# Up weights summed by adding transfers, with plain first blocks, in a two-layer decoder step

## The chip, the cores and the metric

The kernel runs on one core of one Trainium2 chip. It is written instruction by instruction, with semaphores. The metric is the device time of one execution in microseconds: 2723.18 us, the median of three runs (2722.01 to 2725.67).

## The reference, cut to what matters

Two decoder layers are applied to 520 tokens (512 of a prompt, 8 samples), with d_model 1024, all in fp32. Each layer has two FFNs of width 2816, and all four are of this form:

```
h = rmsnorm(x, gain)
x = x + 0.5 * (silu(h @ w1) * (h @ w3)) @ w2
```

Between them stand one input projection, a gated DeltaNet branch, a differential attention branch, a gated merge and an output projection; a per-layer embedding gate ends the layer. The change touches only the FFNs and what prepares x for them, so the rest is left out here.

## The kernel before

**Numbers.** TensorE works on float32r. For full precision each operand is split into a high part (a copy by ACT, rounded to float32r) and a low part (VectorE: value less high), and every product is three matmuls: high x high, high x low, low x high. Activations lie feature by feature on the partitions, so a matmul has a 128 x 128 weight and 260 of the 520 tokens.

**The up stage with seven products.** For one block n of 128 hidden features (22 blocks, KF), w1 and w3 are taken together. Features are cut into an even and an odd half, tokens into two halves: a 2 x 2 by 2 x 2 product. It is computed with seven products and sums of the operands in place of eight (Winograd's form of Strassen). Each product is 4 x 3 = 12 matmuls, so a block is 84 (`up_block`, `up_product`, L730, L742). It needs seven weight matrices of 128 x 512: four arrive (`up_blocks`, L2552) and three or four are sums; and seven matrices of x, sums of the four scaled quarters (`pair_act`, `pair_dve`, L1317 to L1360, into HA and HB).

**One block's way.** `WF[n % 2]` (weven or wodd, L196) holds four slots `w` and three slots `v`. SP loads 1 MB in two transfers (L465) as soon as `split_done` says that block n-2 has its last low part. GpSimd makes two sums (`up_sums`, L1794), VectorE two more (L1907). ACT makes the high parts UHa (in two steps) and UHb (`up_high`, L1386), VectorE the low parts ULa and ULb (`up_low`, L1897); the end of ULb counts `split_done`. TensorE waits for ULa before products 0 and 2 and for ULb before product 4 (`up_waits`, L718). ACT copies partial results out of PSUM (`up_out`, L1405); VectorE adds them to the rest and multiplies by R, the reciprocal root of the norm (`up_u`, `up_v`), ACT applies SiLU, VectorE forms G (`up_g`), ACT its high part and GpSimd its low part (`gate_low`, L1811) for blocks up to 10; for the later ones GpSimd does it after the sums of the last block.

VectorE's order in a block is written out in `ffn` (L1937):

```
up_u(n-1); up_low(n, 2); up_v(n-1); up_low(n+1, 0); up_g(n-1); up_low(n+1, 1); up_sums(n+1)
```

**Start of an FFN.** `up_begin` (L747) runs the first three products of block 0 over feature pairs as x becomes ready, waiting for `hx_raw` and `hx_all`; then comes `norm_sum`, the sum of squares over features by a matmul with ones, and the rest of block 0.

**Down stage.** 16 weight chunks of 128 x 1408 are loaded, split and multiplied with Gh and Gl (L645, `product`); VectorE adds half the result to X.

Of the kernel before, what the change touches and what calls it, by code (L numbers as in the profile page):

```python
# [14 lines left out]
P = 128  # L15
# [127 lines left out]
def hybrid_trunk(nc, A, O):  # L143
    ctx = ExitStack()
    with ctx:
# [37 lines left out]
        acc = at("acc", [P, T], F32, odd_at + 3 * 2048)  # L183
        gap_at = top.at
# [23 lines left out]
        HA, HA0 = (at(n, [P, 8, 4, HT], dt, h_at) for n, dt in (("HA", R32), ("HA0", F32)))  # L208
        HB, HB0 = (at(n, [P, 6, 4, HT], dt, g_at + GE * T * 4) for n, dt in (("HB", R32), ("HB0", F32)))
# [125 lines left out]
        up_sum, up_sum2, up_hi, up_lo, up_form, up_copy = (sem(n) for n in ("up_sum", "up_sum2", "up_hi", "up_lo", "up_form", "up_copy"))  # L335
# [107 lines left out]

        def half_t(c):
            return slice(c * HT, (c + 1) * HT)
# [4 lines left out]
        def _(sp_):  # L450
# [7 lines left out]
            def ffn(L, nb, up, down, hid):  # L458
                for n in range(KF):
                    if n == 1:  # L460
                        sp_.wait_ge(block_done, L * NB + nb + FREE)
                    else:
                        sp_.wait_ge(split_done, L * NB + nb + (n or 1) + 1)
                    for q in range(2):
                        sp_.dma_start(WF[n % 2][q][:, 0:3:2, :],  # L465
                                      up[L, n][:, 1024 * q:1024 * (q + 1)].rearrange("p (a c) -> p a c", a=2)
                                      ).then_inc(raw_ready[n % 2], 16)
                for n in range(2 * KD):
                    sp_.wait_ge(split_done, L * NB + nb + KF + (n if n > 1 else 0) + 1)
                    if n == 1:  # L470
                        sp_.wait_ge(up_sum, 2 * (up_first(L, hid) + KF) - 1)
# [162 lines left out]
        def _(pe):  # L634
# [64 lines left out]
            def norm_sum(L, nj):  # L699

                if L == 0 and nj == 0:
                    pe.wait_ge(loads, 16)
                pe.wait_ge(acc_ready, L * NH + KD * (nj + 1))
                for c in range(2):
                    last = nc.tensor.matmul(ps[:, 6 + c, 0:HT], ones, acc[:, c * HT:(c + 1) * HT], start=True, stop=True)
                last.then_inc(sum_ready, 1)
# [5 lines left out]
            WH = [UHa[:, f, :] for f in range(4)] + [UHb[:, f, :] for f in range(3)]  # L712
            WL = [ULa[:, f, :] for f in range(4)] + [ULb[:, f, :] for f in range(3)]
            XH = [HA[:, 1], HA[:, 0], HA[:, 3], HB[:, 0], HB[:, 1], HA[:, 2], HB[:, 2]]
            XL = [HA[:, 5], HA[:, 4], HA[:, 7], HB[:, 3], HB[:, 4], HA[:, 6], HB[:, 5]]
            BANK = (2, 3, 1, 2, 3, 0, 2)

            def up_waits(L, nb, ub, nj, hid, n, p, f):  # L718
                g = up_first(L, hid)
# [3 lines left out]
                elif f == 2:  # L723
                    pe.wait_ge(up_lo, 2 * n + (2 * g + 2))
                elif f == 4:
                    pe.wait_ge(split_done, n + (L * NB + nb + FREE + 1))
                if f in (3, 4, 6):
                    pe.wait_ge(up_copy, 4 * n + (4 * g + {3: 1, 4: 2, 6: 3}[f]))

            def up_product(p, f, i0=0, i1=4, before=None):  # L730
                for i in range(i0, i1):
                    if before:
                        before(i)
                    w = slice(i * P, (i + 1) * P)
                    for t, (a, x) in enumerate(((WH[f], XH[f]), (WH[f], XL[f]), (WL[f], XH[f]))):
                        last = nc.tensor.matmul(ps[:, 4 * p + BANK[f], 0:HT], a[:, w], x[:, i, :],  # L736
                                                start=f in (0, 1, 2, 5) and i == 0 and t == 0, stop=i == 3 and t == 2,
                                                skip_group_check=True)
                if i1 == 4:
                    last.then_inc(block_done if f == 6 else up_form, 1)  # L740

            def up_block(L, nb, ub, nj, hid, n, p):  # L742
                for f in range(7):
                    up_waits(L, nb, ub, nj, hid, n, p, f)
                    up_product(p, f)

            def up_begin(L, nb, ub, nj, hid):  # L747
                x = 4 * (2 * L + hid)

                def raw_part(i):  # L750
                    pe.wait_ge(hx_raw, x + i + 1)

                def all_part(i):
                    pe.wait_ge(hx_all, x + i + 1)

                for f in range(3):
                    up_waits(L, nb, ub, nj, hid, 0, 0, f)
                    up_product(0, f, 0, 3, all_part if f == 1 else raw_part)
                for f in range(3):
                    up_product(0, f, 3, 4, all_part if f == 1 else raw_part)  # L760
                norm_sum(L, nj)
                for f in range(3, 7):
                    up_waits(L, nb, ub, nj, hid, 0, 0, f)
                    up_product(0, f)
                pe.wait_ge(rt_ready, L * NORMS + (nj + 1))
                up_block(L, nb, ub, nj, hid, 1, 1)

            def ffn(L, nb, ub, nj, hid):
                up_begin(L, nb, ub, nj, hid)
                with pe.Fori(1, KF // 2) as i:  # L770
                    for p in range(2):
                        up_block(L, nb, ub, nj, hid, 2 * i + p, p)
# [505 lines left out]
            for c in range(2):  # L1278
                pe.wait_ge(half_evac2, c + 1)
                pe.wait_ge(acc_ready, DEPTH * NH - 1)  # L1280
                nc.tensor.matmul(ps[:, 6 + c, 0:HT], ones, acc[:, c * HT:(c + 1) * HT], start=True, stop=False)
# [35 lines left out]
        def pair_act(act, L, nj, hid, i):  # L1317

            n = 4 * (2 * L + hid) + i
            if i:  # L1320
                act.wait_ge(hx_all, n)
            for q in range(2):
                nx = nc.scalar.activation(HA0[:, 4 + 2 * q:6 + 2 * q, i, :], halves(X[:, 2 * i + q, :]), ACT.Copy,
                                          scale=gain(L, nj, 2 * i + q))
            nx.then_inc(hx_gain, 1)
            act.drain()
            nc.scalar.activation(HA[:, 1:4, i, :], HA0[:, 5:8, i, :], ACT.Copy).then_inc(hx_hraw, 1)

        def pair_squares(act, L, nj, hid, i):
            act.wait_ge(acc_ready, L * NH + KD * nj + 2 * i)  # L1330
            for q in range(2):
                nc.scalar.activation(ta[:, q, :], X[:, 2 * i + q, :], ACT.Square).then_inc(sq_ready, 1)

        def pair_sums_act(act, L, nj, hid, i):
            act.wait_ge(hx_sum, 4 * (2 * L + hid) + i + 1)
            nc.scalar.activation(HA[:, 0, i, :], HA0[:, 4, i, :], ACT.Copy)
            nc.scalar.activation(HB[:, 0:3, i, :], HB0[:, 3:6, i, :], ACT.Copy).then_inc(hx_hsum, 1)

        def pair_dve(dve, L, nj, hid, i):

            V = nc.vector
            n = 4 * (2 * L + hid) + i + 1
            s1, x11, x22, x12 = (HA0[:, 4 + k, i, :] for k in range(4))
            s2, s4, s3 = (HB0[:, 3 + k, i, :] for k in range(3))
            dve.wait_ge(hx_gain, n)
            V.tensor_tensor(s3, x11, s1, ALU.subtract)
            V.tensor_tensor(s1, s1, x22, ALU.add)
            dve.drain()
            V.tensor_tensor(s2, s1, x11, ALU.subtract)
            dve.drain()  # L1350
            V.tensor_tensor(s4, x12, s2, ALU.subtract).then_inc(hx_sum, 1)
            dve.wait_ge(hx_hraw, n)
            dve.drain()
            V.tensor_tensor(HA[:, 5:8, i, :], HA0[:, 5:8, i, :], HA[:, 1:4, i, :].bitcast(F32), ALU.subtract  # L1354
                            ).then_inc(hx_raw, 1)
            dve.wait_ge(hx_hsum, n)
            dve.drain()
            V.tensor_tensor(HA[:, 4, i, :], s1, HA[:, 0, i, :].bitcast(F32), ALU.subtract)
            V.tensor_tensor(HB[:, 3:6, i, :], HB0[:, 3:6, i, :], HB[:, 0:3, i, :].bitcast(F32), ALU.subtract
                            ).then_inc(hx_all, 1)  # L1360

        def pair_sums_dve(dve, L, nj, hid, i):
            for q in range(2):
                dve.wait_ge(sq_ready, L * NH + KD * nj + 2 * i + q + 1)
                nc.vector.tensor_tensor(acc[:, :], acc[:, :], ta[:, q, :], ALU.add).then_inc(acc_ready, 1)
                dve.drain()

        @block.scalar
        def _(act):
# [9 lines left out]
            def norm_root(L, nj):  # L1379
                act.wait_ge(sum_ready, L * NORMS + (nj + 1))  # L1380
                A_(halves(R[:, :]), pair(6), ACT.Sqrt, scale=1.0 / D, bias=eps).then_inc(rt_ready, 1)
# [3 lines left out]

            def up_high(L, nb, hid, n, g):  # L1386

                b = up_first(L, hid)
                if g == 2:
                    act.wait_ge(block_done, L * NB + nb + n - 1 + FREE + 1)  # L1390
                elif n:
                    act.wait_ge(up_form, 6 * (b + n - 1) + 2 * g + 2)
                else:
                    act.wait_ge(block_done, L * NB + nb + 1)
                if g == 2:
                    act.wait_ge(up_sum2, b + n + 1)
                else:
                    act.wait_ge(up_sum, 2 * (b + n) + g + 1)
# [6 lines left out]
            def up_out(L, nb, nj, hid, n, f):  # L1405

                p = n % 2
                if f == 6:
                    act.wait_ge(block_done, L * NB + nb + n + FREE + 1)
                else:  # L1410
                    act.wait_ge(up_form, 6 * (up_first(L, hid) + n) + f + 1)
                if f == 0:
                    if n < 2:
                        act.wait_ge(acc_ready, L * NH + KD * (nj + 1))
                    else:
                        act.wait_ge(g_ready, up_first(L, hid) + n - 1)
# [1219 lines left out]
```

## Time and profile before

| | us |
|---|---|
| median of 3 runs | 2723.18 |
| profiled execution | 2725.64 |
| its span | 2723.8 |
| TensorE busy | 2603.0 (96%) |
| VectorE busy | 1933.8 (71%) |
| ACT busy | 1185.9 (44%) |
| GpSimd busy | 542.2 (20%) |

Stages of the profiled execution, by the span's clock: FFN 1 from 16.84 (down products from 273.09), FFN 2 to about 1320 (down from 1172), FFN 3 from 1367 (down from 1621), FFN 4 to about 2667 (down from 2520). In the profile an engine's busy time counts its instructions alone; the chain follows the work that ended last; "releaser" names what ended an idle time. VectorE's sums and low parts all have line L1882, a helper, and are told apart by their tiles. A matmul's own duration overlaps the next one's, so the pace of TensorE is read from counts over time.

### The profile page before, as it was taken

To read this page: it belongs to the slowest core of one execution; us is meant where nothing else is said; L and a number is where in the kernel's file an instruction comes from. 1 tells how busy PE (TensorE), PEld (TensorE's weight loads), DVE (VectorE), ACT (ScalarE), POOL (GpSimd) and SP (SyncE) were. 2 spreads that over 40 slices of the span, in tenths; PEclk is the share of its full clock that TensorE was granted. 3 is DMA by queue.
4 is the path that set the end of the run, shared out by engine and by line. 5 is a ranking of instruction groups with operands and counts; after the bars stand their busy time and mean duration, and the time that the engine had idled before them with its cause. 6 is when DMAs were issued, how large, how long until landed. Compare 5 with 4: busy or idle time off the path is not lost.

```text
span 2723.8 us, 54467 instructions
## 1 busy us (share of the span) xinstructions
PE 2603.0 (96%) x22804; PEld 2447.8 (90%) x22804; DVE 1933.8 (71%) x2315; ACT 1185.9 (44%) x1674; POOL 542.2 (20%) x326
## 2 busy tenths in 40 slices
PE   5999999999999899999979999999999998999997
PEld 5999999976699899999969999999757998999997
DVE  7999437665676799953689993476566668999436
ACT  5555323423663555532355552244236535555323
POOL 1432200332000143320024331003220002432300
PEclk9999999999999999999989999999999999999999
DMA  3232332268422123332212232322783222233231
GB/s 106 95 101 99 96 120 99 81 225 285 147 84 88 63 93 100 101 111 83 92 64 93 93 104 97 120 96 94 257 277 107 91 80 69 95 99 106 96 99 64
DMA packets 142109, 304.38 MB, mean 112 GB/s; under 512 B 14946, under 2 KB 25186, under 8 KB 141410
## 3 DMA queue, kind: packets, MB, share of 16 engines
q1 hardware_dynamic: 141922, 301.79, 33.5%
q8 instruction: 129, 2.11, 0.3%
q14 instruction: 58, 0.48, 0.1%
HBM read 290.30 MB, written 11.44 MB: 111 GB/s over the span
## 4 chain that ended last, share of the span: by engine, by line
PE 72%; DVE 14%; DVEq 10%; ACT 2%; issue 2%; ACTq 0%; POOLq 0%
PE ps L645 33%; PE ps L736 14%; PE ps L693 14%; DVEq L1919 4%; DVEq L1925 3%; DVE ta L1882 3%; DVE ULa L1882 2%; DVE tb L1882 2%; PE ps L909 2%; DVEq L1929 2%; DVE G L1882 1%; PE ps L1001 1%; DVE weven L1882 1%; DVE wodd L1882 1%; PE ps L1020 1%
## 5 line engine op out<-in xcount | busy, mean ns | idle before, releaser
L645 PE MATMUL ps<-Gh,ring 128*128 128x260 f32 x2816 | 453.7, 283 | 0.0
L736 PE MATMUL ps<-HA,UHa 128*128 128x260 f32 x2112 | 391.7, 286 | 59.9 <-DVE HA L1354 38.0
L736 PEld LDWEIGHTS ps<-HA,UHa 128*128 128x128 f32 x2112 | 330.2, 191 | 63.1 <-DVE HA L1354 30.5
L645 PEld LDWEIGHTS ps<-Gh,ring 128*128 128x128 f32 x2816 | 386.0, 188 | 0.0
L693 PE MATMUL ps<-Hh,ring 128*128 128x260 f32 x2048 | 342.3, 286 | 0.1
L736 PE MATMUL ps<-HA,ULa 128*128 128x260 f32 x1056 | 301.0, 285 | 0.0
L693 PEld LDWEIGHTS ps<-Hh,ring 128*128 128x128 f32 x2048 | 285.2, 188 | 4.3 <-issue 2.7
L1802 POOL TENSOR_TENSOR weven<-weven,weven 128x512 f32<-128x512 f32 x88 | 136.0, 1546 | 749.8 <-DMA weven<-in_ffn_up 742.7
L645 PE MATMUL ps<-Gl,ring 128*128 128x260 f32 x1408 | 282.6, 282 | 0.0
L736 PE MATMUL ps<-HB,UHb 128*128 128x260 f32 x1408 | 270.3, 289 | 7.1 <-DVE ULb L1882 7.1
L1882 DVE TENSOR_TENSOR ring<-rawd,ring 128x1408 fp32r<-128x1408 f32 x64 | 110.3, 1724 | 190.0 <-ACT ring L1371 190.0
L1371 ACT ACTIVATE ring<-raw 128x2048 fp32r<-128x2048 f32 (+1 forms) x72 | 134.4, 1866 | 236.5 <-PE ps L645 131.9
L736 PEld LDWEIGHTS ps<-HB,UHb 128*128 128x128 f32 x1408 | 218.2, 190 | 14.0 <-DVE ULb L1882 7.4
L1371 ACT ACTIVATE ring<-rawd 128x1408 fp32r<-128x1408 f32 x64 | 88.3, 1380 | 312.5 <-PE ps L645 312.5
L645 PEld LDWEIGHTS ps<-Gl,ring 128*128 128x128 f32 x1408 | 217.3, 188 | 0.0
L1813 POOL TENSOR_TENSOR Gl<-G,Gh 128x520 fp32r<-128x520 f32 x88 | 144.0, 1658 | 341.0 <-ACT Gh L1371 341.0
L693 PE MATMUL ps<-Hl,ring 128*128 128x260 f32 x1024 | 205.7, 282 | 0.0
L736 PEld LDWEIGHTS ps<-HA,ULa 128*128 128x128 f32 x1056 | 202.5, 192 | 0.0
L645 PE MATMUL ps<-Hh,ring 128*128 128x260 f32 x1248 | 201.6, 282 | 0.0
L736 PE MATMUL ps<-HB,ULb 128*128 128x260 f32 x704 | 200.3, 284 | 0.0
L1802 POOL TENSOR_TENSOR wodd<-wodd,wodd 128x512 f32<-128x512 f32 x88 | 137.6, 1563 | 253.7 <-DMA wodd<-in_ffn_up 191.4
L645 PEld LDWEIGHTS ps<-Hh,ring 128*128 128x128 f32 x1248 | 171.0, 188 | 0.2
(322 smaller groups left out, 5617.3 us busy)
## 6 DMA issues: line engine op xcount, KB each, us to landing
weven<-in_ffn_up SPq DMA_DIRECT2D x88, 512.0 KB, 4.7
wodd<-in_ffn_up SPq DMA_DIRECT2D x88, 512.0 KB, 4.9
rawd<-in_ffn_down SPq DMA_DIRECT2D x128, 352.0 KB, 3.4
kb<-in_cache_k SPq DMA_DIRECT2D x128, 256.0 KB, 4.0
kb<-in_cache_v SPq DMA_DIRECT2D x128, 256.0 KB, 4.0
raw<-in_w_in SPq DMA_DIRECT2D x56, 512.0 KB, 4.7
raw<-in_w_gate SPq DMA_DIRECT2D x32, 512.0 KB, 4.6
raw<-in_w_ab SPq DMA_DIRECT2D x16, 512.0 KB, 4.3
```

Of the source, the lines that this page charges most:

```text
L645: last = nc.tensor.matmul(ps[:, bank + 2 * m + c, 0:HT], w, x[:, k0 + k, c * HT:(c + 1) * HT], start=starts and k == 0 and n == 0, stop=st ...
L693: last = nc.tensor.matmul(ps[:, 2 * m + c, 0:HT], w, x[:, k, c * HT:(c + 1) * HT], start=k == 0 and t == 0, stop=k == KD - 1 and t == 2)
L736: last = nc.tensor.matmul(ps[:, 4 * p + BANK[f], 0:HT], a[:, w], x[:, i, :], start=f in (0, 1, 2, 5) and i == 0 and t == 0, stop=i == 3 an ...
L909: last = nc.tensor.matmul(ps[part(h % 2), bank, cell(x, h)], lhs[part(h % 2), cell(x, h)], rhs(part(h % 2), cell(x, h)), start=x == 0 and ...
L1001: last = nc.tensor.matmul(ps[32 * h:32 * h + 32, 6, :].rearrange("p (g k) -> p g k", g=4), qz[:, s * P + 32 * h:s * P + 32 * h + 32], kb[t ...
L1371: return nc.scalar.activation(out, in_, func, **kw)
L1802: nc.gpsimd.tensor_tensor(part_of(o), part_of(a), part_of(b), ALU.subtract).then_inc(up_sum, 1)
L1813: nc.gpsimd.tensor_tensor(Gl[:, n, :], G0[:, n, :], Gh[:, n, :].bitcast(F32), ALU.subtract).then_inc(gl_done, 1)
L1882: return V.tensor_tensor(out, a_, b_, op)
L1919: dve.drain()
L1925: dve.drain()
L1929: dve.drain()
```

## The change

1. The first block of each FFN (the first three of the first FFN) is computed with eight plain products over single feature chunks: `up_plain`, 96 matmuls. x for it is only scaled and split (`raw_act`, `raw_dve`: XR, XT). The sums for the other blocks (HS) are formed beside it (`form_scaled`, `form_sums`, `form_high`, `form_low`).
2. In the other blocks the order and signs of the products change, so that u is complete in PSUM: ACT copies two partial results into other PSUM banks instead of SBUF. `up_u` is one multiplication by R. `up_v` is one operation without R; R is multiplied in after the down products, with the factor -0.5.
3. The weight sums: SP loads the first quarter a second time, into slot `w[:, 1]`. GpSimd then issues two accumulating transfers, which add the fourth quarter to `w[:, 1]` and the third to `v[:, 2]`. VectorE waits for both (`added`) and makes the two other sums, the second from the first. GpSimd makes no weight sums of its own.
4. In VectorE's order `up_sums(n+1)` moves from the end of the block to a place ahead of `up_low(n, 2)`.

The core of the diff:

```
             def ffn(L, nb, up, down, hid):          # SP
                     for q in range(2):
                         sp_.dma_start(WF[n % 2][q][:, 0:3:2, :], ...).then_inc(raw_ready[n % 2], 16)
+                        if q == 0 and n >= plain(L, hid):
+                            sp_.dma_start(WF[n % 2][0][:, 1, :], up[L, n][:, 0:512]).then_inc(first_load[n % 2], 16)
...
+            def add_parts(L, nb, hid, n, up):       # GpSimd
+                w, v = WF[n % 2]
+                pool.wait_ge(raw_ready[n % 2], (L * NB + nb + n) // 2 * 32 + 32)
+                pool.wait_ge(first_load[n % 2], 16 * formed_alike(L, hid, n))
+                pool.dma_start(w[:, 1, :], up[L, n][:, 1536:2048], accum_op=ALU.add).then_inc(added[n % 2], 16)
+                pool.dma_start(v[:, 2, :], up[L, n][:, 1024:1536], accum_op=ALU.add).then_inc(added[n % 2], 16)
+
+            def ffn(L, nb, hid, up):
+                np = plain(L, hid)
+                add_parts(L, nb, hid, np, up)
+                add_parts(L, nb, hid, np + 1, up)
                 for n in range(KF):
-                    up_sums(L, nb, hid, n)
-                    if 2 <= n < GE + 2:
-                        gate_low(L, hid, n - 2)
+                    if 0 < n <= GE:
+                        gate_low(L, hid, n - 1)
+                    if n >= np and n + 2 < KF:
+                        add_parts(L, nb, hid, n + 2, up)
...
+            def up_sums(L, nb, hid, n):             # VectorE
+                w, v = WF[n % 2]
+                dve.wait_ge(added[n % 2], 32 * formed_alike(L, hid, n))
+                TT(w[:, 3, :], w[:, 1, :], v[:, 0, :], ALU.add).then_inc(up_sum, 1)
+                dve.drain()
+                TT(v[:, 1, :], w[:, 3, :], w[:, 2, :], ALU.add).then_inc(up_sum, 1)
...
             def up_u(L, nb, hid, n):
                 done(L, nb + n)
-                dve.wait_ge(up_copy, 4 * (up_first(L, hid) + n) + 4)
-                u = halves(ta[:, n % 2, :])
-                TT(u, pair(4 * (n % 2)), u, ALU.add)
-                dve.drain()
-                TT(ta[:, n % 2, :], ta[:, n % 2, :], R[:, :], ALU.mult).then_inc(ta_ready, 1)
+                TT(halves(ta[:, n % 2, :]), pair(4 * (n % 2)), halves(R[:, :]), ALU.mult).then_inc(ta_ready, 1)
...
             def ffn(L, nb, ub, nj, hid):            # VectorE
                 for n in range(KF):
                     if n:
                         up_u(L, nb, hid, n - 1)
-                    up_low(L, nb, hid, n, 2)
-                    if n:
-                        up_v(L, n - 1)
-                    if n + 1 < KF:
-                        up_low(L, nb, hid, n + 1, 0)
+                        up_v(L, hid, n - 1)
+                        if np <= n + 1 < KF:
+                            up_sums(L, nb, hid, n + 1)
+                    if n >= np:
+                        up_low(L, nb, hid, n, 2)
                     if n:
                         up_g(L, hid, n - 1)
-                    if n + 1 < KF:
-                        up_low(L, nb, hid, n + 1, 1)
-                        up_sums(L, hid, n + 1)
+                    next_low(n + 1, 0)
...
+                    next_low(n + 1, 1)
...
                     if s % 8 > 3:                   # down stage
                         done(L, nb + KF + s)
-                        V.scalar_tensor_tensor(out=halves(Xc(m)), in0=pair(2 * (s % 4)), scalar=0.5, in1=halves(Xc(m)),
+                        TT(halves(dt[:, :]), pair(2 * (s % 4)), halves(R[:, :]), ALU.mult)
+                        dve.drain()
+                        V.scalar_tensor_tensor(out=X[:, m, :], in0=dt[:, :], scalar=-0.5, in1=X[:, m, :],
                                                op0=ALU.mult, op1=ALU.add).then_inc(evac, 1)
```

The plain block on TensorE:

```
+            def up_plain(L, nb, ub, hid, n, h, l, before=None):
+                p = n % 2
+                pe.wait_ge(up_lo, 2 * n + (2 * up_first(L, hid) + 2))
+                pe.wait_ge(split_done, n + (L * NB + nb + FREE + 1))
+                pe.wait_ge(evac, L * NE + n + (ub + 1))
+                for k in range(KD):
...
+                    if before:
+                        before(k)
+                    for m, q in ((0, odd), (1, 3 - odd)):
+                        for t in range(3):
+                            a = l if t == 2 else h
+                            for c in range(2):
+                                x = xs[c][t == 1]
+                                last = nc.tensor.matmul(ps[:, 4 * p + 2 * m + c, 0:HT], a[:, q, w], x[:, i, :],
+                                                        start=k == 0 and t == 0, stop=k == KD - 1 and t == 2)
```

TensorE's waits for ULa and ULb stay at products 0, 2 and 4.

## Rows read from the trace of the kernel before

**Rows 1.** Page: busy time and share of each engine, and the chain by engine.
```profile
PE 2603.0 (96%) x22804; PEld 2447.8 (90%) x22804; DVE 1933.8 (71%) x2315; ACT 1185.9 (44%) x1674; POOL 542.2 (20%) x326
...
PE 72%; DVE 14%; DVEq 10%; ACT 2%; issue 2%; ACTq 0%; POOLq 0%
```

**Rows 2.** TensorE's waits over the span: us in total, times, longest.
```profile
PE ps L736 <- DVE HA L1354: 38.0, 9, 9.6
PE ps L736 <- ACT ta L1371: 30.0, 39, 1.1
PE ps L736 <- DVE ULa L1882: 16.8, 1, 16.8
PE ps L736 <- DVE ULb L1882: 7.1, 4, 2.6
```

**Rows 3.** The chain in order of time: start, us, what.
```profile
40.70 8.25 PE ps L736 x48
...
127.04 2.63 DVEq L1919
138.33 2.62 DVEq L1919
149.57 2.63 DVEq L1919
...
165.39 107.70 PE ps L736 x888
```

**Rows 4.** Windows: stretch, its us, then busy us (count) of PE, PEld, DVE, ACT, POOL; PEclk, DMA, GB/s.
```profile
60.00:165.00 105.00, 97.78 (x784) 94.63 (x782) 102.59 (x94) 54.30 (x83) 45.74 (x29) 1.00 0.28 90
165.00:273.00 108.00, 107.61 (x889) 107.21 (x890) 103.70 (x107) 56.28 (x86) 26.64 (x18) 1.00 0.31 101
273.00:410.00 137.00, 137.00 (x1143) 136.97 (x1142) 52.14 (x46) 42.14 (x48) 20.41 (x12) 1.00 0.34 112
```

**Rows 5.** Timeline of VectorE and GpSimd, 114 to 120 us: start, us, what.
```profile
114.61 1.56 POOL L1813 TENSOR_TENSOR Gl<-G,Gh 128x520 fp32r<-128x520 f32 x1 [6.31 <-ACT Gh L1371]
114.91 3.50 DVE L1882 TENSOR_TENSOR wodd<-wodd 128x512 f32<-128x512 f32 x2
...
119.09 1.03 DVE L1882 TENSOR_TENSOR ta<-ta,R 128x520 f32<-128x520 f32 x1
120.05 1.74 DVE L1882 TENSOR_TENSOR ULb<-wodd,UHb 128x1536 fp32r<-128x1536 f32 x1
```

**Rows 6.** Timeline of all engines, 194 to 209 us.
```profile
194.51 2.85 DVE L1882 TENSOR_TENSOR ULb<-weven,UHb 128x1536 fp32r<-128x1536 f32 x1
...
197.38 0.88 SPq L465 DMA_DIRECT2D weven<-in_ffn_up  x2
...
201.74 1.29 DVE L1882 TENSOR_TENSOR wodd<-wodd 128x512 f32<-128x512 f32 x2
...
202.61 1.57 POOL L1802 TENSOR_TENSOR weven<-weven,weven 128x512 f32<-128x512 f32 x1 [6.87 <-DMA weven<-in_ffn_up]
...
204.34 1.56 POOL L1802 TENSOR_TENSOR weven<-weven,weven 128x512 f32<-128x512 f32 x1 [0.16 <-issue]
...
205.27 1.05 ACT L1371 ACTIVATE UHa<-weven 128x1024 fp32r<-128x1024 f32 x1
...
208.14 1.06 ACT L1371 ACTIVATE UHa<-weven 128x1024 fp32r<-128x1024 f32 x1
```

**Rows 7.** TensorE's waits from 16 to 48 us, then from 1362 to 1396.
```profile
PE ps L736 <- DVE HA L1354: 11.7, 3, 7.2
...
PE ps L736 <- DVE HA L1354: 20.0, 4, 9.6
```

**Rows 8.** Windows at the starts of FFN 1 and FFN 3.
```profile
16.84:48.00 31.16, 17.70 (x82) 15.66 (x83) 26.56 (x40) 19.05 (x30) 2.35 (x2) 0.84 0.11 34
...
1367.00:1394.00 27.00, 15.63 (x80) 14.22 (x81) 19.63 (x31) 16.93 (x25) 2.59 (x2) 0.63 0.12 40
```

**Rows 9.** Timeline of TensorE at the start of FFN 2.
```profile
931.72 0.51 PE L736 MATMUL ps<-HA,UHa 128*128 128x260 f32 x2 [3.09 <-DVE HA L1354]
934.02 0.80 PE L736 MATMUL ps<-HA,UHa 128*128 128x260 f32 x2 [1.67 <-DVE HB L1359]
```

**Rows 10.** GB/s in 40 slices of the window 195 to 217 us.
```profile
GB/s 0 0 0 0 0 0 134 294 130 331 402 402 212 0 0 0 0 0 0 0 0 0 0 0 45 220 246 220 358 402 331 86 0 0 0 0 0 0 0 0
```

**Rows 11.** DMA issues over the span: count, KB each, median us to landing.
```profile
kb<-in_cache_k SPq DMA_DIRECT2D x128, 256.0 KB, 4.0
...
raw<-in_w_ple SPq DMA_DIRECT2D x8, 256.0 KB, 2.9
```

More of the change, by code:

```diff
@@ L442, in up_first, with plain, formed, formed_alike @@
             return (2 * L + hid) * KF
+        def plain(L, hid):
+            return 1 if L or hid else 3
+        def formed(L, hid, n):
+            return sum(KF - plain(*f) for f in ((0, 0), (0, 1), (1, 0))[:2 * L + hid]) + n - plain(L, hid)
+        def formed_alike(L, hid, n):
+            return sum(len(range(plain(l, h), n + 1 if (l, h) == (L, hid) else KF)[(n - plain(l, h)) % 2::2])
+                       for l, h in ((0, 0), (0, 1), (1, 0), (1, 1))[:2 * L + hid + 1])
         def half_t(c):
@@ L742, in up_block @@
-            def up_block(L, nb, ub, nj, hid, n, p):
+                last.then_inc(block_done if f == 6 else up_form, 1)
+            def up_block(L, nb, ub, hid, n, p, before=None):
                 for f in range(7):
-                    up_waits(L, nb, ub, nj, hid, n, p, f)
+                    up_waits(L, nb, ub, hid, n, f)
+                    if before and f == 1:
+                        before()
                     up_product(p, f)
[L747 to L760, printed above, removed]
-                norm_sum(L, nj)
[L762 to L766, printed above, removed]
@@ new lines, in square_act, with square_dve, staged @@
+        def square_act(act, L, nj, m):
+            if m > 1:
+                act.wait_ge(acc_ready, L * NH + KD * nj + m - 1)
+            nc.scalar.activation(ta[:, m % 2, :], X[:, m, :], ACT.Square).then_inc(sq_ready, 1)
+        def square_dve(dve, L, nj, m):
+            dve.wait_ge(sq_ready, L * NH + KD * nj + m + 1)
+            nc.vector.tensor_tensor(accu[:, :], accu[:, :], ta[:, m % 2, :], ALU.add).then_inc(acc_ready, 1)
+            dve.drain()
+        def staged(L, hid, i):
+            return SS[i][:, :, :] if L and not hid and i < 3 else HS0[:, 4:8, i, :]
@@ L1824, in _ @@
             for L in range(DEPTH):
-                ffn(L, 0, 0)
+                ffn(L, 0, 0, A["ffn1_up"])
                 pool.wait_ge(split_done, L * NB + (46 + FREE))
@@ L1937, in ffn, with next_low @@
             def ffn(L, nb, ub, nj, hid):
+                np = plain(L, hid)
+                def next_low(n, g):
+                    if n < np:
+                        plain_low(L, nb, hid, n, g)
+                    elif n < KF:
+                        up_low(L, nb, hid, n, g)
+                if np == 1:
+                    form_sums(dve, L, hid, 3)
+                    up_sums(L, nb, hid, 1)
                 for n in range(KF):
```

379 lines of the change are left out of this document (218 added, 161 removed).

## The prediction

> **What bounds the kernel now.** I read the page's shares first: TensorE works 96% of the span, VectorE 71%, and the chain that ended last is 72% TensorE and 24% VectorE or its queue [rows 1]. So most stages end on TensorE and a quarter of the chain is something else. The list of TensorE's waits says where: `ps L736`, the up products of the FFNs, waits for `HA`, `ta`, `ULa`, `ULb` [rows 2]; the down products of L645 hardly wait at all.
>
> Inside an up stage there are two regimes. In the chain, the same VectorE step (the wait of L1919) comes back every 11.28 us in FFN 1 (127.04, 138.33, 149.57), and from 165.39 the chain is TensorE alone [rows 3]. By the windows, 60 to 165 us has 784 products where 165 to 273 has 889, with VectorE at 98% against 96% [rows 4]. A block is 84 products; in the TensorE regime that is 84 x 108/889 = 10.2 us, that is 0.1215 us a product. In the slow regime VectorE runs without a pause, and its two sums take 3.50 us together [rows 5] against 1.29 us in the fast one [rows 6]: GpSimd also reads SBUF then, since blocks up to 12 carry its `Gl` step of 1.56 us beside its two sums [rows 5].
>
> The third thing is the buffer loop of the weights. SP issues the load of block n+2 when `ULb` of block n is done: `ULb` starts at 194.51 and takes 2.85, the load is issued at 197.38, and GpSimd, waiting for it, starts the sums at 202.61 [rows 6]. That is 5.23 us from issue to use. The sums end at 204.2 and 205.9; ACT takes them up at 205.27 and 208.14 [rows 6], so this loop has 1 to 2 us of slack today.
>
> **The change, part by part.**
>
> *Plain first blocks.* Block 0 of each FFN (blocks 0 to 2 in the first) takes 8 k x 2 x 3 x 2 = 96 products in place of 84: 6 blocks x 12 x 0.12 = +8.6 us.
>
> *Stage starts.* The plain block takes x feature by feature, so it needs only the scaled copy and its low part, not the seven formed sums. Before, FFN 1 waits 11.7 us for `HA` between 16 and 48 us [rows 7], and 31.2 us pass with 17.7 busy at a granted clock of 0.84 [rows 8]. FFN 3 waits 20.0 us for `HA` and has a clock of 0.63 in 1367 to 1394 [rows 7, 8]. FFNs 2 and 4 lose 3.1 + 1.7 at this point [rows 9]. After: ACT needs about 0.65 us a feature chunk for the copy and 0.6 for the square, so FFN 1's block 0 is fed at TensorE's pace and ends near 31 instead of 49 (40.70 + 8.25 [rows 3]). I take 15 us for FFN 1, 18 for FFN 3 (the sums for block 1 are still late by some 5 us there), 4 each for FFNs 2 and 4: -41 us, between -20 and -55.
>
> *u completed in PSUM, v left unscaled.* VectorE loses two multiplies by R a block (0.70 and 1.03 [rows 5]), GpSimd loses its two sums, and with these their collisions. VectorE's work is then 0.69 + 0.69 + 1.4 + 1.75 + 0.70 + 1.22 + 1.22 = 7.7 us a block, under TensorE's 10.2. About 10 blocks in each of 4 FFNs fall from 11.28 to 10.2: -44 us. R is multiplied in after the down products instead: 8 more operations of 0.69 a FFN, beside products, since VectorE is busy 52.1 of 137 us there [rows 4]. Only the last of each FFN is bare: +3 us. The extra lifts of ACT are as many as before.
>
> So without the transfers: 8.6 - 41 - 44 + 3 = -73 us.
>
> *The accumulating transfers.* Two sums go from GpSimd arithmetic to transfers. The chain for block n+2 is now: SP issues three loads (one more, 256 KB); both semaphores full; GpSimd issues two adding transfers of 256 KB; both land; VectorE makes two sums, the second from the first; only behind them, in VectorE's order, stands `ULb` of block n+1 (in the new `ffn`, `up_sums(n + 1)` comes ahead of `up_low(n, 2)`); and its end releases the load of block n+3. This is a closed loop, once around for each block: nothing in it runs beside anything else in it. Queued behind VectorE's wait for `added` are `ULb`, then the silu product and both `ULa`; TensorE waits for `ULb` at its fifth product, after 48 of 84. On GpSimd the `Gl` step of block n-1 stands ahead of the issue; its input comes about 2 us after the release and it takes 1.56, so it is over before the load lands. On SP nothing else is queued.
>
> The length of one turn, T:
> - load: 5.23 us now [rows 6]; the third transfer adds 0.44 of issue (two take 0.88) and 0.26 MB of data, about 0.65 us at the 402 GB/s that the window peaks at [rows 10]; these partly overlap: 5.8 us.
> - the pair of adds, A: no adding transfer and no transfer issued by GpSimd is in the trace. From below, one plain transfer of 256 KB lands in 2.9 us (`raw<-in_w_ple`) [rows 11]. From above, twice the load pair, 10.4. An add fetches its source and its target, so the two fetch 1 MB, as the load pair does; I take that pair's 5.2 us.
> - two dependent sums: 1.4 us (1.29 for two independent ones [rows 6]); `ULb` 1.75 [rows 5], with no GpSimd arithmetic beside it; semaphore hops 0.2.
>
> T = 5.8 + A + 1.4 + 1.75 + 0.2 = 9.15 + A: 14.35 us for A = 5.2, 12.05 for 2.9, 19.55 for 10.4. All lie above 10.2, so TensorE idles T - 10.2 in each turn. Turns: from the last plain block's `split_done` to block 20's, less the first, which starts with loads already in hand: 17 in FFN 1, 19 in each of the others, 74. That is 74 x 4.15 = +307 us (137 to 692).
>
> Idle gaps of 4 us can lower the clock: after waits of 3.09 and 1.67 us a pair of products takes 0.80 instead of 0.51 [rows 9], the 1.2 GHz level. At that level the 36 products behind `ULb` take 7.7 us, and VectorE's two PSUM reads end 9.3 us after the release, when the load and the adds (11.0) are still out. So it costs nothing, unless A is as low as 2.9, and then 0.6 a turn.
>
> Sum: 2725.6 (the profiled execution; its span is 2723.8) - 73 + 307 = 2959 us. The median of the runs is 2.5 us under the profiled execution, so 2957.
>
> **Two rules of the Trainium skill.** The row for the nearest plain transfer gives 2.9 us for 256 KB [rows 11]. The Trainium skill, "DMA: Bandwidth & Descriptors", Anatomy of one DMA — SWDGE (gpsimd) path, puts a GpSimd-issued transfer at about 2.0 us fixed plus its bytes over 436 GB/s; as an estimate, the pair would land in 3.2 us, T be 12.35 and the time 2809. The Trainium skill, "Collectives: The Full Stack", The bandwidth ceiling: the fold count and why AG ≠ RS ≠ AR, says a summing transfer moves at half the rate of a copy, because it reads two sources; no row here shows an add, and it leans to the longer price.
>
> **Rivals.**
> - *Cheap adds (0.17).* The pair behaves as small plain transfers do, 2.7 to 3.9 us: T of 11.8 to 13, time 2771 to 2857. For it: 2.9 us in rows 11. Against: issue, fetch of the target and order of the two come on top. (This is where the first rule above would put it.)
> - *Dear adds (0.23).* The adding path is slower for each byte, or GpSimd needs microseconds to issue: A over 7.4, T over 16.5, time over 3118; at A = 10.4 it is 3344. Against: four times 256 KB of cache pages, issued together, land in 4.0 us [rows 11]. For it: nothing in the trace shows this path at all.
> - *Hidden transfers (0.06).* Faster. If the turn is under 10.2 us the transfers are off the path and only the -73 stays: 2652. That needs the adds to be out of the loop. The time crosses today's at T = 11.2, A = 2.0, less than any load of this size takes [rows 11]; so it needs my reading of VectorE's order or of the load's release to be wrong.
> - *A draw (0.02).* T between 11.1 and 11.3.
>
> **How the numbers follow.** The forecast, T of 13 to 16.5, has 0.52: 2857 to 3118, at 2957. The range takes in both bounds of A, 2780 to 3340. What this kernel's measurements can tell from no change is about 0.2%. Slower: 0.52 + 0.17 + 0.23 = 0.92; within 0.2%: 0.02; faster: 0.06.
>
> **What would show it.** In the up stages the chain should turn every 14.35 us, with VectorE's wait for the adding transfers in it and TensorE waiting about 4 us for `ULb`, once a block, in 74 turns. The issue-to-landing time of the new transfers gives A directly. Down stages should last as before. The first TensorE waits of FFN 1 and FFN 3 for `HA` should be gone. Forecast wrong if blocks come at 10.2 us (the loop is not closed as I read it), if the time is over 3340 (an add costs more than two plain megabytes), or if the starts did not shrink.

## The result, and the profile after

| | before | after |
|---|---|---|
| median, us | 2722.6 (2720.83 to 2725.67) | 3141.38 (3136.15 to 3147.54, 4 runs) |
| profiled execution, us | 2725.64 | 3137.87 |
| its span, us | 2723.8 | 3136.1 |

The ratio is 1.1535 (95% interval 1.1512 to 1.1559): slower by 15%. The forecast was 2957 us, slower. The direction and the place were right, and the loss is 419 us where 234 were forecast.

The page of the changed kernel: busy time by engine, then two rows of DMA queues (packets, MB, share of 16 engines' span), then the shares of the chain by engine. They stand against [rows 1].

```profile
PE 2752.4 (88%) x22876; PEld 2599.3 (83%) x22876; DVE 1697.7 (54%) x2153; ACT 1187.3 (38%) x1660; POOL 411.1 (13%) x314
...
q1 hardware_dynamic: 153730, 323.29, 32.3%
q0 software_dynamic: 23616, 43.00, 8.4%
...
PE 53%; DMA 28%; DVE 7%; DVEq 5%; SPq 2%; issue 2%; POOL 1%; ACT 1%; ACTq 0%
```

TensorE falls from 96% to 88%, though its busy time rises by 149 us (2603.0 to 2752.4) for only 72 more products: its clock is lower, as the windows below show. DMA, which had no visible share of the chain, now has 28%. VectorE and GpSimd did get less to do, as the change says (1933.8 to 1697.7, 542.2 to 411.1): neither is the bound. TensorE's waits (us in total, times, longest) say where its idle time lies; they answer to [rows 2].

```profile
PE ps L761 <- DVE ULb L1968: 307.1, 77, 5.5
...
PE ps L793 <- DVE PWl L1968: 20.0, 1, 20.0
...
PE ps L761 <- DVE ULa L1968: 9.9, 2, 5.6
...
PE ps L793 <- ACT R L1435: 9.1, 1, 9.1
```

The waits for `HA` are gone. One wait makes up most of TensorE's idle time (307 of 384 us): 77 times, for `ULb`, some 4 us each. Behind it stands one turn of the weight loop. The rows of SP, GpSimd, VectorE and TensorE that bear on it (start, us, what, idle before and its releaser):

```profile
153.30 1.75 DVE L1968 TENSOR_TENSOR ULb<-weven,UHb 128x1536 fp32r<-128x1536 f32 x1
155.08 0.37 SPq L487 DMA_DIRECT2D weven<-in_ffn_up  x1
155.18 0.80 PE L761 MATMUL ps<-HS,UHb 128*128 128x260 f32 x2 [4.23 <-DVE ULb L1968]
...
155.49 0.47 SPq L491 DMA_DIRECT2D weven<-in_ffn_up  x1
156.00 0.43 SPq L487 DMA_DIRECT2D weven<-in_ffn_up  x1
...
156.60 1.54 POOL L1887 TENSOR_TENSOR Gl<-G,Gh 128x520 fp32r<-128x520 f32 x1 [8.85 <-ACT Gh L1435]
...
162.10 0.88 POOL L1895 DMA_DIRECT2D weven<-in_ffn_up  x1 [3.96 <-DMA weven<-in_ffn_up]
162.68 1.19 POOL L1896 DMA_DIRECT2D weven<-in_ffn_up  x1
...
168.57 0.69 DVE L1968 TENSOR_TENSOR weven<-weven,weven 128x512 f32<-128x512 f32 x1 [5.36 <-DMA weven<-in_ffn_up]
169.35 0.69 DVE L1968 TENSOR_TENSOR weven<-weven 128x512 f32<-128x512 f32 x1
169.96 1.75 DVE L1968 TENSOR_TENSOR ULb<-wodd,UHb 128x1536 fp32r<-128x1536 f32 x1
171.74 0.37 SPq L487 DMA_DIRECT2D wodd<-in_ffn_up  x1
```

From 155.08 to 171.74 is one turn, 16.66 us. The three loads are issued at 155.08, 155.49 (the added one) and 156.00; GpSimd, which is past its `Gl` step by 158.14, waits another 3.96 us for them and issues the adds at 162.10 and 162.68; VectorE waits 5.36 us until they land, makes the two sums, then the *other* buffer's `ULb` (`wodd`), and only that frees the buffer for the next load. What costs is that `ULb` of the block in hand, for which TensorE waits, is queued behind VectorE's wait for the next block's adds.

Over the up stages, the ends of `ULb` give 74 such turns (17 and three times 19) with a mean of 16.38 us, where the kernel before has 11.28 and then 10.16. Two windows of it, in the form of [rows 4]: one in the up stage of FFN 1, one in its down stage.

```profile
100.00:340.00 240.00, 182.90 (x1230) 179.74 (x1229) 112.17 (x118) 81.81 (x122) 33.94 (x34) 0.82 0.46 113
...
368.00:490.00 122.00, 122.00 (x1018) 122.00 (x1017) 47.29 (x45) 37.26 (x43) 19.63 (x12) 1.00 0.31 101
```

The up stage has 1230 products in 240 us (0.195 us each, where [rows 4] give 0.1215); the down stage runs as before, 137.07 us in the chain for what took 136.79. The trace's clock splits the 412 us by which the span grew: from the first `ULb` of a block with sums to that of block 20 the four FFNs take 1212 us for 795 before (+417), the starts up to that first `ULb` gain 14, and the stretch from `ULb` of block 20 to the first down product loses 9. So the loss is in the up stages.

### The profile page after: what moved, and what is told of

It reads as the page before. It is cut to its first block, busy times and chain, and to the rows that moved or that the text cites. A ratio compares the mean times of both kernels' runs of the same rounds, so it can differ in the third digit from the quotient of the medians.

```text
span 3136.1 us, 54284 instructions
## 1 busy us (share of the span) xinstructions
PE 2752.4 (88%) x22876; PEld 2599.3 (83%) x22876; DVE 1697.7 (54%) x2153; ACT 1187.3 (38%) x1660; POOL 411.1 (13%) x314
## 3 DMA queue, kind: packets, MB, share of 16 engines
q1 hardware_dynamic: 153730, 323.29, 32.3%
q0 software_dynamic: 23616, 43.00, 8.4%
## 4 chain that ended last, share of the span: by engine, by line
PE 53%; DMA 28%; DVE 7%; DVEq 5%; SPq 2%; issue 2%; POOL 1%; ACT 1%; ACTq 0%
PE ps L669 29%; DMA wodd<-in_ffn_up 16%; DMA weven<-in_ffn_up 13%; PE ps L717 12%; DVEq L2026 4%; PE ps L954 2%; DVE wodd L1968 2%; DVE weven L1968 2%; PE ps L761 2%; SPq L491 1%; PE ps L1046 1%; SPq L487 1%; PE ps L793 1%; POOL wodd L1895 1%; PE ps L1094 1%
## 5 line engine op out<-in xcount | busy, mean ns | idle before, releaser
L761 PE MATMUL ps<-HS,UHb 128*128 128x260 f32 x1312 | 387.6, 396 | 307.1 <-DVE ULb L1968 307.1
L761 PEld LDWEIGHTS ps<-HS,UHb 128*128 128x128 f32 x1312 | 322.4, 298 | 323.3 <-issue 314.7
L717 PEld LDWEIGHTS ps<-Hh,ring 128*128 128x128 f32 x2048 | 285.1, 188 | 4.6 <-issue 2.7
L761 PE MATMUL ps<-XR,UHa 128*128 128x260 f32 x1312 | 245.7, 285 | 9.9 <-DVE ULa L1968 9.9
L761 PE MATMUL ps<-HS,ULb 128*128 128x260 f32 x656 | 251.4, 383 | 0.0
L761 PE MATMUL ps<-HS,UHa 128*128 128x260 f32 x1312 | 242.5, 285 | 0.0
L761 PEld LDWEIGHTS ps<-XR,UHa 128*128 128x128 f32 x1312 | 204.0, 190 | 10.7 <-DVE ULa L1968 10.7
L761 PEld LDWEIGHTS ps<-HS,UHa 128*128 128x128 f32 x1312 | 204.0, 190 | 0.4 <-DVE HS L1429 0.2
L761 PEld LDWEIGHTS ps<-HS,ULb 128*128 128x128 f32 x656 | 194.2, 296 | 0.0
L761 PE MATMUL ps<-XR,ULa 128*128 128x260 f32 x656 | 186.5, 284 | 0.0
```

The source lines that it names most:

```text
L717: last = nc.tensor.matmul(ps[:, 2 * m + c, 0:HT], w, x[:, k, c * HT:(c + 1) * HT], start=k == 0 and t == 0, stop=k == KD - 1 and t == 2)
```

## The experiments

All times are medians beside the kernel before on the same chip (2720.9 to 2725.0 us there). "A turn" is the mean distance of the ends of `ULb` in the 74 turns.

### What the adding transfers cost against GpSimd arithmetic

e1 keeps every other part of the change and makes the same two sums with GpSimd instructions.

```
-   if q == 0 and n >= plain(L, hid):
-       sp_.dma_start(WF[n % 2][0][:, 1, :], up[L, n][:, 0:512])
...
-   pool.dma_start(w[:, 1, :], up[L, n][:, 1536:2048], accum_op=ALU.add)
-   pool.dma_start(v[:, 2, :], up[L, n][:, 1024:1536], accum_op=ALU.add)
+   nc.gpsimd.tensor_tensor(w[:, 1, :], w[:, 0, :], v[:, 2, :], ALU.add)
+   nc.gpsimd.tensor_tensor(v[:, 2, :], v[:, 2, :], v[:, 0, :], ALU.add)
```

> The changed kernel, but GpSimd makes the two sums with arithmetic (two tensor_tensor in place of the two adding transfers, no third load). Theory (the adding transfers close a loop of 16.4 us a block, and that is all the loss): blocks come at 10.2 us; 74 turns x (16.37 - 10.2) = 457 us come off 3141, so 2685 us, and FFN 1 and 2 start as slowly as in the changed kernel. Rival (the adds also hold up the starts of the FFNs, where the changed kernel gained only 13 us of the 41 forecast): 2652 us. Rival (something else in the change, its plain blocks or the R multiply in the down stage, costs part): above 2723.

Measured: 2765.93 us, ratio 1.0162 (1.0143 to 1.0182), a turn of 11.43 us. The transfers cost 375 us of the 419. But without them the kernel is still slower than before, the last case of the expectation, and the -73 us of my sum is not there. TensorE's wait and the turn in the timeline show why:

```profile
PE ps L759 <- DVE ULb L1966: 88.8, 75, 4.3
```

```profile
154.73 0.88 SPq L487 DMA_DIRECT2D weven<-in_ffn_up  x2
...
160.05 1.29 POOL L1892 TENSOR_TENSOR weven<-weven,weven 128x512 f32<-128x512 f32 x1 [2.24 <-DMA weven<-in_ffn_up]
...
161.50 1.29 POOL L1894 TENSOR_TENSOR weven<-weven 128x512 f32<-128x512 f32 x1 [0.16 <-issue]
...
162.83 0.69 DVE L1966 TENSOR_TENSOR weven<-weven,weven 128x512 f32<-128x512 f32 x1 [2.08 <-POOL weven L1894]
...
164.22 1.75 DVE L1966 TENSOR_TENSOR ULb<-wodd,UHb 128x1536 fp32r<-128x1536 f32 x1
...
166.00 0.88 SPq L487 DMA_DIRECT2D wodd<-in_ffn_up  x2
```

Load 5.32, two sums on GpSimd 2.78, VectorE 3.17: 11.27 us, the same closed loop with a shorter middle. (In the medians over the turns the load takes 5.5 here and 7.1 in the changed kernel, the middle 2.8 and 6.1: of the 5 us that the transfers add to a turn, 1.6 are the third load and 3.3 the adds.) It is closed by the order on VectorE (`up_sums(n+1)` ahead of `up_low(n, 2)`), whoever makes the sums.

### Which part of an adding transfer costs

e2 replaces the two adds by plain copies of the same bytes to the same place (two of the four sums are left out); e3 also moves their issue from GpSimd to SP; e4 keeps the adds but on 128 of the 512 columns (three quarters of two sums are left out).

```
-   pool.dma_start(w[:, 1, :], up[L, n][:, 1536:2048], accum_op=ALU.add)
e2: pool.dma_start(w[:, 1, :], up[L, n][:, 1536:2048])
e3: sp_.dma_start(WF[n % 2][0][:, 1, :], up[L, n][:, 1536:2048])
e4: pool.dma_start(w[:, 1, 0:128], up[L, n][:, 1536:1664], accum_op=ALU.add)
    (and the same for the second of the pair)
```

> The changed kernel with the two GpSimd transfers as plain copies of the same bytes (the two sums are left out: the slots get the copied quarter). Theory (an adding transfer moves at half the rate because it reads its target too: 163 GB/s against 319 by the queue rows): the pair's 512 KB take 1.6 us in place of 3.2, a turn 14.8 us, the time 3023. Rival (the price is the way over GpSimd's issue, not the adding): a turn stays at 16.4 and the time at 3141.

> As the kernel with plain copies, but SP issues them, after waiting for the block's loads (the two sums are left out). Theory (GpSimd's issue and path cost about 1.5 us of each turn besides the adding): a turn of 13.4 us, 2920 us. Rival (only the adding is dear): the same as with copies issued by GpSimd.

> The changed kernel with adding transfers of 128 of the 512 columns (three quarters of both sums are left out). Theory (of the 6.5 us from GpSimd's issue to VectorE's sum 3.2 are data at 163 GB/s, the rest fixed): 2.4 us off a turn, 14.0 us, 2963 us. Rival (the 6.5 us are fixed cost of the two issues): a turn of 16.2 us, 3130 us.

| | us | ratio (95%) | a turn | middle part, from its issue to VectorE's sum, median |
|---|---|---|---|---|
| after: adds | 3141.38 | 1.1535 (1.1512 to 1.1559) | 16.38 | 6.1 |
| e2: copies, GpSimd | 2990.96 | 1.0994 (1.0972 to 1.1016) | 14.48 | 4.2 |
| e3: copies, SP | 2949.3 | 1.0841 (1.0819 to 1.0863) | 13.94 | 3.9 |
| e4: quarter adds | 2959.08 | 1.0877 (1.0853 to 1.09) | 13.94 | 3.6 |

e2 and e4 came near what was expected of them (14.8 and 14.0 us a turn). e3 missed: 13.4 us was expected from 1.5 us for GpSimd's issue and path, and these turn out to be 0.5. The rows of e2, the queue of the copies and one pair in the timeline:

```profile
q0 software_dynamic: 13120, 43.00, 4.8%
...
wodd<-in_ffn_up POOLq DMA_DIRECT2D x86, 256.0 KB, 3.5
```

```profile
168.16 0.55 POOL L1895 DMA_DIRECT2D wodd<-in_ffn_up  x1 [4.09 <-DMA wodd<-in_ffn_up]
...
172.55 0.69 DVE L1968 TENSOR_TENSOR wodd<-wodd,wodd 128x512 f32<-128x512 f32 x1 [4.02 <-DMA wodd<-in_ffn_up]
```

The landing time of an add in the changed kernel (the row of its queue stands above), then both rows of e4, a quarter of the bytes:

```profile
wodd<-in_ffn_up POOLq DMA_DIRECT2D x86, 256.0 KB, 5.1
```

```profile
q0 software_dynamic: 23616, 10.76, 3.0%
...
wodd<-in_ffn_up POOLq DMA_DIRECT2D x86, 64.0 KB, 3.0
```

What follows: the adding itself costs 1.9 us a turn (16.38 against 14.48), GpSimd's issue path only 0.5 (14.48 against 13.94), shared between a later start after the load (7.1 against 6.8 us from the load's issue) and a longer middle (4.2 against 3.9). Three quarters of the added bytes are worth 6.1 - 3.6 = 2.5 us, so as an estimate the pair of adds is 3.3 us of data and 2.8 fixed. The largest part of the excess over 10.2 is neither: it is that a load and then a second round of transfers stand one behind the other in a loop that nothing overlaps.

### The order on VectorE

e5 is e1 with one move, e6 is the changed kernel with the same move.

```
-                        if np <= n + 1 < KF:
-                            up_sums(L, nb, hid, n + 1)
                     if n >= np:
                         up_low(L, nb, hid, n, 2)
+                    if n and np <= n + 1 < KF:
+                        up_sums(L, nb, hid, n + 1)
```

> Sums by GpSimd arithmetic as in the first experiment, and VectorE's order changed: ULb of block n ahead of the sums of block n+1. Theory (VectorE's order closes the loop whoever adds: load 5.2 + GpSimd 2.8 + sums and ULb 3.15 = 11.3 us; with ULb first, the loop goes over two blocks and TensorE's 10.2 us decide): 74 x 1.2 = 89 us off 2766, 2677 us, faster than both kernels. Rival (collisions of VectorE and GpSimd set the 11.4 us): stays within 15 us of 2766.

> The changed kernel with its adding transfers, only VectorE's order changed as above. Theory: the loop over VectorE goes over two blocks, but ACT still waits for the next block's adds (UHa of n+1) ahead of the lift that TensorE's product 4 of block n needs; block n+1's adds land 13.3 us after the release, so two blocks take 14.8 + 4.4 + 3.4 = 22.6 us, 11.3 a block, 74 x 5 = 375 us off: about 2766. Rival (the transfers' length counts in full on any path): above 3000. Rival (ACT's order does not matter): 2685.

e5: 2656.89 us (2656.22 to 2659.37, 5 runs), ratio 0.9766 (0.9752 to 0.9779), a turn of 10.04. It beats both kernels. Its busy times, a window in the up stage of FFN 1, and what is left of the wait for `ULb`:

```profile
PE 2576.8 (97%) x22876; PEld 2438.6 (92%) x22876; DVE 1721.0 (65%) x2153; ACT 1190.8 (45%) x1660; POOL 490.5 (18%) x314
```

```profile
100.00:240.00 140.00, 140.00 (x1172) 140.00 (x1171) 105.80 (x112) 78.91 (x117) 44.40 (x33) 1.00 0.32 105
```

```profile
PE ps L759 <- DVE ULb L1966: 8.5, 3, 2.9
```

1172 products in 140 us are 0.1195 us each, without a pause: 88.8 us of waits have become 8.5. The move is worth 109 us with GpSimd's sums.

e6: 2848.57 us (2838.35 to 2855.62), ratio 1.0454 (1.0425 to 1.0484), a turn of 12.49: 293 us less than the changed kernel, and 83 more than expected. Its turns mostly alternate, about 10 and about 15 us. Part of the 83 is that the transfers of the two buffers now overlap: the load takes 7.8 us in the median and the middle 6.6, where the changed kernel has 7.1 and 6.1. The releaser has changed, and ACT's timeline says what ACT does meanwhile:

```profile
PE ps L761 <- ACT tb L1435: 118.9, 44, 4.8
```

```profile
222.67 1.06 ACT L1435 ACTIVATE UHa<-weven 128x1024 fp32r<-128x1024 f32 x1 [3.90 <-DMA weven<-in_ffn_up]
...
223.64 0.37 ACT L1435 ACTIVATE tb<-ps 128x260 f32<-128x260 f32 x1
```

The same fault, one engine on: the lift `tb` (a copy by ACT of a partial result out of its PSUM bank) of the block in hand stands behind `UHa` of the next, which waits 3.90 us for its transfers.

### The order on ACT

e7 is e6 with the lifts to PSUM ahead of `UHa(n+1)` on ACT, the last of them only ahead of `UHb(n+1)`; e9 has all of them ahead.

```
-                    next_high(n + 1, 0)
+                    if n < np:
+                        next_high(n + 1, 0)
...
                     if 0 < n <= GE:
                         gate_high(L, hid, n - 1)
+                    if n >= np:                      e7: next_high, then up_out(.., 4)
+                        up_out(L, hid, n, 4)         e9: up_out(.., 4), then next_high
+                        next_high(n + 1, 0)
                     next_high(n + 1, 1)
...
-                    if n >= np:
-                        up_out(L, hid, n, 4)
```

> As before, with ACT's order changed too: in formed blocks the lifts of PSUM come ahead of the high parts that wait for the next block's adds. Theory: no engine waits for an add ahead of work that TensorE needs sooner; blocks come at 10.2 to 10.5 us, 2685 to 2705 us, and the adding transfers are hidden. Rival (ACT's order does not matter, or its later high parts now are late): same as with VectorE's order alone.

> The adding transfers, ULb first on VectorE, and on ACT all three lifts of a block ahead of the high parts that wait for the next block's adds (in the run before, the lift for product 6 still stood behind them, and TensorE waited 101 us for it). Theory (closed orders, not the transfers, are what is left): blocks come near 10.3 us with short waits for ULa, 2690 to 2720 us. Rival (the adds, landing about 13.5 us after their buffer's release, are late by themselves for the two buffers): 2780 us or more, with the waits moved from ACT to ULa.

e7: 2800.44 us (2796.43 to 2811.85), ratio 1.0285 (1.0268 to 1.0302), a turn of 11.91. Missed, by 95 us and more, though 48 us faster than e6: the one lift that I left behind `UHa` took over the wait.

```profile
PE ps L761 <- ACT ps L1435: 101.3, 46, 5.2
```

e9: 2801.93 us (2797.15 to 2808.03), ratio 1.0287 (1.0259 to 1.0315), a turn of 11.85. The theory missed again, by 80 us and more, and the rival's time holds: now the transfers themselves are late. The waits moved to `ULa` only in part; 39.7 us are still for a lift.

```profile
PE ps L761 <- DVE ULa L1970: 62.5, 49, 5.5
...
PE ps L761 <- ACT ps L1435: 39.7, 24, 4.4
```

```profile
203.87 0.37 SPq L487 DMA_DIRECT2D weven<-in_ffn_up  x1
...
211.68 0.86 POOL L1897 DMA_DIRECT2D weven<-in_ffn_up  x1 [10.14 <-DMA weven<-in_ffn_up]
...
217.88 0.69 DVE L1970 TENSOR_TENSOR weven<-weven,weven 128x512 f32<-128x512 f32 x1 [3.82 <-DMA weven<-in_ffn_up]
...
221.42 0.51 PE L761 MATMUL ps<-XR,UHa 128*128 128x260 f32 x2 [0.94 <-DVE ULa L1970]
```

Load 7.81 and adds 6.20 in this turn: 14 us from the release of a buffer to its use, and then two sums and `ULa` of that block before TensorE can begin it.

e10 is e9 with the adds as plain copies (two of the four sums are left out).

```
-   pool.dma_start(w[:, 1, :], up[L, n][:, 1536:2048], accum_op=ALU.add)
+   pool.dma_start(w[:, 1, :], up[L, n][:, 1536:2048])      (and the second)
```

> The same orders with plain copies in place of the adding transfers (both sums are left out). Theory: if the adds are hidden, making them 1.9 us shorter changes little, under 20 us. Rival: if they are still late, up to 1.9 us for each of two blocks, 40 to 80 us less than with adds.

e10: 2684.29 us, ratio 0.9858 (0.9833 to 0.9883), a turn of 10.37; 14.9 us of waits for `ULa` in place of 62.5, and 3.7 for the lift in place of 39.7, so those waits too were owed to the adds. It is 118 us less than e9, more than the theory (under 20) and the rival (40 to 80) allowed.

```profile
PE ps L761 <- DVE ULa L1970: 14.9, 19, 3.5
...
PE ps L761 <- ACT ps L1435: 3.7, 4, 1.2
```

What follows: the adds are not hidden even when no in-order queue closes the loop over one block. In the medians the load and the adds take 8.2 and 6.5 us (e9), the load and the copies 7.1 and 4.2: 3.4 us a way. 2.3 of them are the adds' own; 1.1 are in the load, which the rival had not counted. One way serves two blocks, since there are two buffers, which makes 1.7 a block; the difference of the two kernels, 118 us over 74 turns, is 1.6. A third buffer wasn't tried.

### The start of FFN 1

e8 is e5 with the norm's root ahead of the forming of `HS` on ACT, since TensorE waits there 8.0 us for `R` (9.1 in the changed kernel).

```
                     next_high(n + 1, 1)
+                    if np > 1 and n == 0:
+                        norm_root(L, nj)
                     if np > 1 and n < 2:
...
-                    if n == 0:
+                    if np == 1 and n == 0:
                         norm_root(L, nj)
```

> Sums by GpSimd arithmetic, ULb first, and in the first FFN the root of the norm ahead of the forming of HS on ACT. Theory (TensorE's 9.1 us wait at the start of block 1 is for the root, which stands in ACT's queue behind two formings): 7 us less than with ULb first alone. Rival (the second table load or later forms take it back): no difference.

Measured: 2661.11 us (2658.82 to 2663.06), ratio 0.978 (0.9765 to 0.9796): no gain over e5's 2656.89. TensorE's timeline:

```profile
34.84 0.39 PE L791 MATMUL ps<-XT,UHa 128*128 128x260 f32 x1 [0.79 <-ACT R L1433]
...
54.85 0.56 PE L791 MATMUL ps<-XT,PWh 128*128 128x260 f32 x1 [8.24 <-DVE PWl L1968]
```

The wait for `R` fell to 0.79 us and came back 20 us later as 8.24 for `PWl`, a low part of VectorE that stands behind the formed sums.

## Why the prediction was right, and where it was not

**Mechanism: right.** The closed loop through SP, GpSimd, the adding transfers and VectorE's order, once a block, 74 turns, TensorE waiting about 4 us for `ULb`, down stages untouched: all as written. The profiled execution can be made up from it: 2725.6, + 457 for 74 x (16.38 - 10.2), and -45 for the rest, is 3137.9. The 45 can be read from the two traces: -14 at the starts, -41 for the 74 turns of the kernel before (795 us, where 74 x 10.2 is 755), +9 at the ends of the up stages. The forecast had 178 us less: 150 of them are the turn, 28 this rest, which stood there as -73.

**The length of the turn: 16.38 instead of 14.35, +150 us.** By its terms:

| | forecast | measured |
|---|---|---|
| load (median) | 5.8 | 7.1 |
| adds A (median) | 5.2 | 6.1 |
| sums, `ULb`, hops | 3.35 | 3.17 |

The load failed in two places. Its base of 5.23 was one pair's: the median from issue to GpSimd's start is 5.6 in the kernel before and 5.5 in e1. And where I said "these partly overlap", the third load adds 1.6 us (e1's 5.5 to 7.1), *more* than the sum of my 0.44 and 0.65. The issue is as priced: the last load starts 0.5 us later for it (the row of 155.49). Nearly all of the other 1.1 us is in the transfers, for 256 KB more on 1 MB: the last of them lands 6.8 us after the first issue, in e1 5.3. Why they take more than the 0.65 of the window's peak rate was not tested.

A was sized by the bytes that an add must fetch, and the load pair as its copy. The rate fits an add that reads its target as well: 43.00 MB take 8.4% of 3136.1 us (163 GB/s) as adds and 4.8% of 2988.9 us (300 GB/s) as copies in e2. It is near the half rate that the Trainium skill, "Collectives: The Full Stack", The bandwidth ceiling: the fold count and why AG ≠ RS ≠ AR, gives to the reducing transfers of a ReduceScatter, which read two sources; this case's traces agree (1.84 times). But the load pair was a poor copy: it lands in 5.3 us, the pair of adds in 6.1. GpSimd's issue can explain only a little of that: its second add starts 0.58 us after the first, SP's second load 0.41, and the copies' middle part is 0.3 us shorter when SP issues them (e3). What makes up the rest is open. The rule that I did weigh, the Trainium skill, "DMA: Bandwidth & Descriptors", Anatomy of one DMA — SWDGE (gpsimd) path, estimated the pair at 3.2 us: even plain copies take 4.2 (e2), and adds 6.1. The measurement decides against it here.

**The starts: -14 instead of -32.** The forecast was -41, with 8.6 us for the plain blocks on top; together they make 18 of the 28 us. The other 10 are small: the ends of the up stages (+9, with only 3 us forecast for anything behind the up stages), and 41 instead of 44 us for the slow regime. From the beginning of an up stage (in FFN 1 of the span) to the first `ULb` of a block with sums the gain is 4, -1, 10 and 0 us for FFNs 1 to 4. "If the starts did not shrink" was one of my signs of a wrong forecast, and for FFNs 2 and 4 it is met. In FFN 1 TensorE's first product comes at 20.01 us where it came at 16.84, and the waits for `HA` gave way to one for `R`:

```profile
43.28 0.59 PE L793 MATMUL ps<-XT,UHa 128*128 128x260 f32 x1 [9.13 <-ACT R L1435]
```

In FFN 2 (and in 4, 4.3 us) block 1 waits for its weights:

```profile
1038.50 0.80 PE L761 MATMUL ps<-XR,UHa 128*128 128x260 f32 x2 [5.58 <-DVE ULa L1968]
```

I priced the starts by what the formed sums cost before, and didn't follow the adds into them. In FFNs 2 and 4 this stretch takes 27.5 us in the kernel before, 28.4 and 27.2 in the changed one, and 23.6 and 23.5 in e1, which differs from it only in the adds and the third load: these ate what the plain blocks gained. (In e5, with `ULb` first as well, it is 22.2 and 22.1.) The name of what is late next (R in ACT's queue) was readable from the diff; e8 shows that moving it alone only passes the wait on.

**"Without the transfers -73 us": the step that failed in its reasoning, though it did not move the total.** I gave the loop's length to the adds and took for granted that the kernel without them would run at TensorE's pace. e1 says +44 us instead. The same order on VectorE that I had named as what closes the loop closes it with GpSimd's sums too, at 5.3 + 2.8 + 3.2 = 11.3 us, over 10.2; I had written that the crossing is at T = 11.2 and did not put the arithmetic version in. With the order mended (e5) the change brings -66 us, near the -73, though by other parts: its trace, 69 us shorter than that of the kernel before, has -27 us at the starts, -52 in the 74 turns (743 us for 795) and +11 at the ends of the up stages. The steps one after another: from before to e5 -66, the order on VectorE +109 (e1), the transfers +375 (after). The order in which one takes them matters: with the move made first, the transfers cost 192 (e6 against e5).

**The clock: right.** After 59 of the 76 waits of over 2 us for `ULb` a pair of products takes 0.80 us (as at 155.18, the 1.2 GHz level), and the granted clock is 0.82 in the window of the up stage, 0.924 over the span. The slower products hide behind the adds: VectorE has read both of TensorE's results 8.2 us after the release in the median (9.3 forecast), and the adds let it go on only 13.2 us after it.

**The rivals.** Hidden transfers and the draw fell with the first row of waits. Cheap adds fell with A = 6.1 (and with 4.2 even for copies). Dear adds is missed by its condition (A over 7.4, T over 16.5) and met by its time: 3141 us lies above the 3118 to which I had given 0.52, because a turn of 16.38 is just under that border and the rest fell 28 us short. So the time is not where I put the most weight; it is inside the range as a whole, which took in every A from 2.9 to 10.4, and that it held owes more to this width than to my A.

## What to carry to other kernels

Before an arithmetic step is handed to a transfer, draw the loop that frees its buffer, in the order of each in-order queue, and ask which op of the block in hand is queued behind a wait for the next block: one such op on VectorE cost 109 us here, and 293 with the slower transfers. Put the instruction that frees a buffer ahead of the one that waits for the next buffer's data, on every engine of the loop; when it is done on one, read the waits again, for the next engine may have the same fault (e6, e7: it had here). And a load with adding transfers behind it is two full waits in a row, 7.1 + 6.1 us here, where a load and two GpSimd instructions take 5.5 + 2.8.

## What the runs showed of the hardware

- Adding transfers move at 163 GB/s where plain ones of the same size and place have 300 (e2) and the loads 319 (q1: 323.29 MB in 32.3% of 3136.1 us); one of 256 KB lands in 5.1 us against 3.5, one of 64 KB still in 3.0, and the packets are 23616 for 13120.
- GpSimd's rows for the issue of the two adds last 0.88 and 1.19 us (they overlap: 0.58 us from start to start), those of the copies 0.55 each; issued by SP the first of the pair is 0.33. As a whole GpSimd's path costs 0.5 us a turn (e2 against e3). One pair of e3, whose 4.25 us is longer than the median of 3.9:

```profile
163.18 0.33 SPq L495 DMA_DIRECT2D wodd<-in_ffn_up  x1
...
167.43 0.69 DVE L1969 TENSOR_TENSOR wodd<-wodd,wodd 128x512 f32<-128x512 f32 x1 [5.10 <-DMA wodd<-in_ffn_up]
```

- A load of 256 KB between two of 512 KB puts 1.5 us on the time until all have landed (5.3 to 6.8, medians of e1 and the changed kernel), of which its issue is 0.5.
- Adds slow a load that runs beside them: in e9 the three loads have landed after 8.0 us where adds of the other buffer are in flight (71 of 78) and after 7.0 where none are; in e6 the two are 8.4 and 6.8 us. Beside plain copies the difference is small, 6.85 against 6.7 (e10).
